# Second layer of a two-layer decoder: merged outputs kept in the query tiles, five rotating homes for cache keys and values, merges spread over the decode batches, residual split tile by tile

## What is computed

```python
def combine_groups(outs, lses):
    wts = jax.nn.softmax(jnp.stack(lses, axis=0), axis=0)
    return jnp.einsum('gnts,gntsd->ntsd', wts.astype(outs[0].dtype), jnp.stack(outs, axis=0))
```

## Time and profile before

| | |
|---|---|
| median of 3 runs | 2571.18 us (2569.72 to 2571.59) |
| the profiled execution | 2568.12 us |
| its span, first to last instruction | 2566.3 us |
| busy: PE, PEld, DVE, ACT, POOL | 2458.2, 2369.6, 1005.3, 657.2, 366.7 us |
| mean granted TensorE clock | 0.988 of full |
| DMA | 186.7 MB, mean 73 GB/s |
| stretch from the first sample score to oB | 1561.88 to 1702.56 us |

### The profile page before, as it was taken

One profiled execution on the slowest core, in us unless ns is written; L12 is line 12 of the kernel. 1 busy time (PEld: TensorE's weight loads), 2 busy tenths in 40 slices (PEclk: granted clock), 3 DMA queues, 4 the chain that ended last, 5 costly groups with the idle time before them and its releaser, 6 DMA issues. The chain is left out here.

```text
span 2566.3 us, 41256 instructions
## 1 busy us (share of the span) xinstructions
PE 2458.2 (96%) x16803; PEld 2369.6 (92%) x16803; DVE 1005.3 (39%) x1911; ACT 657.2 (26%) x1247; POOL 366.7 (14%) x242
## 2 busy tenths in 40 slices
PE   8999899999999999999999997689999999999997
PEld 8887799999999999999999775479999999999997
DVE  6566536322332232236212485436322322323235
ACT  4345324211110111123100493124211111111123
POOL 4333101101100101101111202201101100100100
PEclk9999999999999999999999999899999999999999
DMA  4011214113111313111211233523113111311312
GB/s 173 21 52 36 69 50 141 43 37 120 41 39 56 101 34 121 42 36 49 91 66 35 99 106 102 188 93 115 49 36 107 53 35 47 114 32 54 111 34 85
DMA packets 64943, 186.72 MB, mean 73 GB/s; under 512 B 11288, under 2 KB 17816, under 8 KB 64056
## 3 DMA queue, kind: packets, MB, share of 16 engines
q1 hardware_dynamic: 63928, 180.46, 21.7%
q0 software_dynamic: 912, 4.85, 0.5%
HBM read 175.85 MB, written 44.70 MB: 86 GB/s over the span
## 5 line engine op out<-in xcount | busy, mean ns | idle before, releaser
L969 DVE TENSOR_TENSOR WL<-RAW,WH 128x1024 fp32r<-128x1024 f32 (+3 forms) x196 | 216.4, 1105 | 1147.7 <-ACT WH L632 1147.1
L1508 PE MATMUL PS<-XH,WH 128*128 128x384 f32 x2832 | 621.0, 329 | 5.5 <-DVE XL L996 3.2
L1508 PE MATMUL PS<-XH,WL 128*128 128x384 f32 (+1 forms) x2736 | 603.5, 328 | 0.0
L1508 PE MATMUL PS<-XL,WH 128*128 128x384 f32 x2640 | 581.7, 328 | 0.0
L1508 PEld LDWEIGHTS PS<-XH,WH 128*128 128x128 f32 x2832 | 484.0, 188 | 7.3 <-issue 4.3
L632 ACT CAST WH<-RAW 128x1024 fp32r<-128x1024 f32 (+3 forms) x196 | 184.8, 944 | 1164.0 <-PE PS L1508 1149.1
L1508 PEld LDWEIGHTS PS<-XH,WL 128*128 128x128 f32 x2736 | 467.6, 188 | 0.0
L496 POOL TENSOR_TENSOR RAW<-RAW,GAIN 128x1024 f32<-128x1024 f32 x112 | 225.9, 2019 | 1663.7 <-DMA RAW<-in_w_gu 1418.7
L1508 PEld LDWEIGHTS PS<-XL,WH 128*128 128x128 f32 x2640 | 450.7, 188 | 0.0
L1508 PE MATMUL PS<-HL,WH 128*128 128x384 f32 (+1 forms) x1041 | 228.6, 327 | 0.0
L1508 PE MATMUL PS<-HH,WL 128*128 128x384 f32 (+1 forms) x1041 | 228.5, 327 | 0.0
(11 more groups left out here) (222 smaller groups left out, 2355.5 us busy)
## 6 DMA issues: line engine op xcount, KB each, us to landing
RAW<-in_w_gu SPq DMA_DIRECT2D x88, 512.0 KB, 3.5
out_bkS<-in_bk_in SPq DMA_DIRECT2D x8, 2032.0 KB
out_bvS<-in_bv_in SPq DMA_DIRECT2D x8, 2032.0 KB
RAW<-in_w_dn SPq DMA_DIRECT2D x32, 384.0 KB, 3.0
KC<-in_bk_in SPq DMA_DIRECT2D x8, 1536.0 KB, 10.9
VC<-in_bv_in SPq DMA_DIRECT2D x8, 1536.0 KB, 7.6
RAW<-in_w_dn SPq DMA_DIRECT2D x32, 320.0 KB, 2.9
XT<-in_xT SPq DMA_DIRECT2D x16, 544.0 KB, 4.8
```

Source lines behind the costliest of these rows:

```text
L969: nc.vector.tensor_tensor(lo[:, j, 0:nk * P], RAW[:, j, 0:nk * P], hi[:, j, 0:nk * P].bitcast(F32), ALU.subtract).then_inc(S["wl"], 1)
L1508: ins = mm(PS[:, 3 * j + c, 0:width], w[:, j, k * P:(k + 1) * P], x(k, a, width), start=(k == 0 and n == 0), stop=(k == nk - 1 and n == 2))
```

## The change

- The twelve tiles of QB grow from 1024 to 1088 columns; QNB goes, and the sample queries stand in the last 64 columns of their query tile. QBR is the same memory as fp32r. The key area moves up by 3072 bytes.
- The merged outputs are no longer written to XH. For a head pair p the tiles of groups 1 and 2 take the high and the low part once their products have been added (`outputs(QBR, 1)` and `outputs(QBR, 2)`); the sample outputs go to their last 64 columns. oB reads them there (`part(1)`, `part(2)`).
- KC and VC of all batches rotate through five homes outside the query tiles: KC0, VC0, KC1, VC1, ... take home 0, 1, 2, 3, 4, 0, ... Loads from the sixth on wait for the scores or values of the batch that used the home (`sb_pv` b-2 for keys, `sb_s` b-1 for values). VC0 and KC1 are asked for when the values of call C2 are done, VC1 and KC2 when the prompt's attention is done.
- The order by hand becomes one loop over the 8 batches on each engine. Batch b carries merge unit (b // 2, b % 2), the two rows of groups 0 and 1 before its values and the third behind them. `merge_hi` and `merge_lo` take a whole head pair (1024 columns) every second batch, the last pair after the loop.
- The TSN copies go; the mask is read from TSW at a constant offset.
- oB's slabs make XH and XL tile by tile (`split=True`); `after_o` isn't called for it, `release` isn't either, and both next slabs are prefetched.
- DVE waits for its own copy of VNB before it goes on to the queries.

```diff
@@ tiles
-        QB = at("QB", [P, 12 * SEQ], R)
-        KB = at("KB", [P, 4 * SEQ], R + 49152)
-        QNB = at("QNB", [P, 12, NEW], R + 65536)
+        QB = at("QB", [P, 12 * TOK], R)
+        QBR = at("QBR", [P, 12 * TOK], R, F32R)
+        KB = at("KB", [P, 4 * SEQ], R + 52224)
...
-        TSN = at("TSN", [P, NG, NEW], R + 79872)
-
-        KC = [at("KC0", [P, 4, KEPT], R + 49152), at("KC1", [P, 4, KEPT], o_wh + 4096), at("KC2", [P, 4, KEPT], R + 12288)]
-        VC = [at("VC0", [P, 6, 512], o_xl), at("VC1", [P, 6, 512], R), at("VC2", [P, 6, 512], R + 24576)]
+
+        HOMES = (R + 52224, o_xh + 16384, o_xl, o_wh + 4096, o_xh)
+        KC = [at(f"KC{b}", [P, 4, KEPT], HOMES[2 * b % 5]) for b in range(NEWB)]
+        VC = [at(f"VC{b}", [P, 6, 512], HOMES[(2 * b + 1) % 5]) for b in range(NEWB)]
...
+        def outputs(x, part):
+
+            return x[:].rearrange("p (a g n) -> p a g n", a=4, g=NG)[:, :, part]
@@ SP
+            def cache_in(n):
+
+                x, src = (KC, keys_of) if n % 2 == 0 else (VC, values_of)
+                sp.dma_start(x[n // 2][:], src(n // 2)).then_inc(S[f"home{n % 5}"], 16)
...
             sp.wait_ge(S["score"], C2)
-            values_in(0)
+            sp.wait_ge(S["pv"], C2)
+            cache_in(1)
+            cache_in(2)
             sp.wait_ge(S["ttr"], 64)
             sp.dma_start(TSB[:], t["tabSB"]).then_inc(S["tsb"], 16)
...
             sp.wait_ge(S["tr"], 2 * C3)
             sp.wait_ge(S["pv"], C3)
-            keys_in(1)
-            sp.wait_ge(S["sb_s"], 1)
-            keys_in(3)
-            sp.wait_ge(S["sb_pv"], 1)
-            values_in(3)
-            sp.wait_ge(S["c_lo"], 2)
-            values_in(1)
-            sp.wait_ge(S["c_lo"], 4)
-            keys_in(2)
-            sp.wait_ge(S["c_lo"], 6)
-            values_in(2)
-            for b in range(4, NEWB):
-                sp.wait_ge(S["sb_s"], b - 2)
-                keys_in(b)
-                sp.wait_ge(S["sb_pv"], b - 2)
-                values_in(b)
+            cache_in(3)
+            cache_in(4)
+            for n in range(5, 2 * NEWB):
+                b = n // 2
+                if n % 2 == 0:
+                    sp.wait_ge(S["sb_pv"], b - 2)
+                else:
+                    sp.wait_ge(S["sb_s"], b - 1)
+                cache_in(n)
             slabs("oB", t["w_oB"])
@@ POOL
+            for b in range(NEWB):
+                if b + 2 < NEWB:
+                    sample(b + 2)
+                pool.wait_ge(S["sb_stage"], 2 * min(b + 3, NEWB))
+                add(b // 2, b % 2)
+                pool.wait_ge(S["c_add"], 2 * b + 2)
@@ ACT
+            for b in range(NEWB):
                 if b + 1 < NEWB:
                     sample(b + 1)
-                if b + 1 == NEWB:
-                    act.wait_ge(S["sb_s"], NEWB)
+                sample_keys(b)
+                sample_norm(b)
+                if b and b % 2 == 0:
+                    merge_hi(b // 2 - 1)
+                sample_out(b)
+                if b == NEWB - 2:
+                    act.wait_ge(S["sb_pv"], NEWB - 1)
                     act.wait_ge(S["rows_out"], 80)
                     start("oB")
-                sample_keys(b)
-                sample_norm(b)
-                sample_out(b)
-            t_phase("oB", evac_sq(3, "oB"))
-            after_o(3, "oB")
+            merge_hi(3)
+            t_phase("oB", evac_sq(3, "oB", split=True))
@@ DVE
+            for b in range(NEWB):
                 if b + 1 < NEWB:
                     sample(b + 1)
-                if b + 1 == NEWB:
+                else:
                     start("oB")
+                    merge_product(b // 2, b % 2, 0)
+                    merge_product(b // 2, b % 2, 1)
+                sample_keys(b)
                 sums(b)
-                sample_keys(b)
+                for g in range(NG):
+                    if b + 1 < NEWB or g == 2:
+                        merge_product(b // 2, b % 2, g)
                 sample_out(b)
+                if b and b % 2 == 0:
+                    merge_lo(b // 2 - 1)
+            merge_lo(3)
             dve.wait_ge(S["rows_out"], 80)
-            t_phase("oB", evac_res(3, late=True), peel=True)
-            after_o(3, "oB")
+            t_phase("oB", evac_res(3, split=True), peel=True)
+            add_squares(3, KT - 1, 1)
+            low(3, KT - 1)
@@ PE
+            for b in range(NEWB):
+                p, h = b // 2, b % 2
                 if b + 1 < NEWB:
                     sample_scores(b + 1)
-                sample_turn(b)
+                    sample_turn(b)
+                    merge_row(p, h, 0)
+                    merge_row(p, h, 1)
+                else:
+                    merge_row(p, h, 0)
+                    merge_row(p, h, 1)
+                    sample_turn(b)
                 sample_values(b)
+                merge_row(p, h, 2)
                 sample_out(b)
-            pe.wait_ge(S["c_lo"], 8)
+            pe.wait_ge(S["c_lo"], 4)
             pe.wait_ge(S["sb_ol"], 16)
-            t_phase("oB", tiles(XH), tiles(XH, 4), None, release=True)
+            part = lambda z: lambda k, a, n: QBR[:, (NG * k + z) * TOK + a:(NG * k + z) * TOK + a + n]
+            t_phase("oB", part(1), part(2), None)
```

More of the change, by code:

```diff
@@ L640, in pair @@
                             split_hi(name, 2 * i + j + 2, j)
-                        elif prefetch and PLAN.next(name) and not (j and name in ("oA", "oB")):
+                        elif prefetch and PLAN.next(name) and not (j and name == "oA"):
                             split_hi(PLAN.next(name), j, j)
@@ L1340, in coefficients, with merge_product, merge_lo @@
                 ins.then_inc(S["coef"], 1)
-            def merge_products(p, h):
-                for g in range(NG):
-                    n = 3 * (2 * p + h) + g
-                    dve.wait_ge(S["c_t"], n + 1)
-                    x = natural(g, p, h)
-                    nc.vector.tensor_tensor(x, x, as_tokens(PS[:, 2 * (n % 2), :], g), ALU.mult).then_inc(S["c_mul"], 1)
-            def merge_lo(p, h):
-                n = 2 * p + h
-                dve.wait_ge(S["c_hi"], n + 1)
-                at, to = q_at(0, p) * SEQ + 512 * h, p * TOK + 512 * h
-                nc.vector.tensor_tensor(XH[:, 4 * TOK + to:4 * TOK + to + 512], QB[:, at:at + 512],
-                                        XH[:, to:to + 512].bitcast(F32), ALU.subtract).then_inc(S["c_lo"], 1)
+            def merge_product(p, h, g):
+                n = 3 * (2 * p + h) + g
+                dve.wait_ge(S["c_t"], n + 1)
+                x = natural(g, p, h)
+                nc.vector.tensor_tensor(x, x, as_tokens(PS[:, 2 * (n % 2), :], g), ALU.mult).then_inc(S["c_mul"], 1)
+            def merge_lo(p):
+                dve.wait_ge(S["c_hi"], p + 1)
+                nc.vector.tensor_tensor(outputs(QBR, 2)[:, p, 0:SEQ], outputs(QB, 0)[:, p, 0:SEQ],
+                                        outputs(QBR, 1)[:, p, 0:SEQ].bitcast(F32), ALU.subtract).then_inc(S["c_lo"], 1)
             dve.wait_ge(S["tsb"], 32)
@@ L1873, in sample_scores, with merge_row @@
                 ins.then_inc(S["sb_s"], 1)
-            def merge_rows(p, h):
+            def merge_row(p, h, g):
                 pe.wait_ge(S["coef"], 1)
-                for g in range(NG):
-                    n = 3 * (2 * p + h) + g
-                    if n >= 2:
-                        pe.wait_ge(S["c_mul"], n - 1)
-                    for x in range(4):
-                        for kk in range(2):
-                            c = CW[:, g, 4 * h + x, 2 * p + kk:2 * p + kk + 1].to_broadcast([P, HD])
-                            ins = mm(PS[64 * kk:64 * kk + 64, 2 * (n % 2), x * P:(x + 1) * P], c, IDN[:], start=True, stop=True)
-                    ins.then_inc(S["c_t"], 1)
+                n = 3 * (2 * p + h) + g
+                if n >= 2:
+                    pe.wait_ge(S["c_mul"], n - 1)
+                for x in range(4):
+                    for kk in range(2):
+                        c = CW[:, g, 4 * h + x, 2 * p + kk:2 * p + kk + 1].to_broadcast([P, HD])
+                        ins = mm(PS[64 * kk:64 * kk + 64, 2 * (n % 2), x * P:(x + 1) * P], c, IDN[:], start=True, stop=True)
+                ins.then_inc(S["c_t"], 1)
             def sample_turn(b):
```

143 lines of the change are left out of this document (21 added, 122 removed).

## The result

The kernel after takes 2527.41 us (median of 4 runs, 2525.73 to 2531.24) beside 2571.39 for the kernel before (4 runs, 2569.72 to 2572.30): ratio 0.983, 95% interval 0.9817 to 0.9842. The prediction was 2527.7 us. The profiled execution is one of 2526.71 us, with a span of 2524.9 and a mean clock of 0.994 (before 2568.12, 2566.3 and 0.988).

What follows compares the result with a forecast made beforehand. PE is busy 96% of the span, so only its waits before oB and behind it can give time. Terms: -40.1 + 0.6 - 4.0 = -43.5 from 2568.12, so 2524.6, median 2527.7 us; range 2521 to 2541.

Steps and rivals of the forecast that it cites:

- What bounds the stage: First sample score to oB: loads and products make PE wait; afterwards PE's own work fills each step, 10.9 us.
- The two delays of 1.25 us: Steps of batches 2 and 4: `merge_lo`, behind a POOL addition, delays the next minima; 2.5 us in all.
- Step 7: Last batch: two rows 1.98, turn to values 4.06, values 1.87, third row 0.99; 8.9 us.
- 6, where the next step asks for no minima: Batch 6: `merge_lo` there was to delay nothing, as no minima follow; 0 us.
- Step 0: First batch, from scores(0) at 1561.88 to the next step's start at 1580.0, with 0.5 us for the clock.
- End chain: Behind the last third row, PE waits for product, addition, `merge_hi`, `merge_lo` and hops before oB; 5.7 us.
- The ramp: Start of oB: after 5 us idle it may run longer at the lower clock; +0.6 us, bounds 0 and 4.
- The seam: oB's end to gu10's first slab: with the residual split tile by tile nothing is lost; -4.0 us, bounds -4 and 0.
- no idle time behind XL: gu10's first slab: a sign of being right, PE not waiting there for XL tiles.
- load took the place of the merge wait: Rival, scores 3 to 7: keys land late, steps of 16.6 or 13.3 us, time 2556 or 2540; chance 0.08.
- The chain: Rival, steps: hops between rows and products and POOL overlaps cost +7, 2535; no own chance, counted in the forecast's range.
- the lower clock: Rival, whole stage: PE at 1.2 GHz, 2597 us, chance 0.04; for two or three steps 2538 to 2548, chance 0.06.

Runs made afterwards that it cites:

- the old seam: Kernel after with the end of oB as before (no tile-by-tile split, `after_o` and `release` back, second slab not prefetched): 2529.81 us, ratio 0.9836.
- second set of runs: Kernel after, unchanged, five runs on one chip beside the version with all repairs: 2530.18 us, ratio 0.9840.

## Why the prediction was right, point by point

**What bounds the stage.** Right. Before, the loads waited for merges and the merges for products; with both waits gone PE's own work is the step (busy 10.64 of 10.82 us; 10.9 predicted). That the keys have 12.2 us from request to use and that this is enough was right; shifted by one step it is not, as the late requests show. One sign was set wrong: PE was to be busy above 90% of the stage, and nearly the 96.5 us of before. It was busy 85.63 us, 86%. The prediction's own waits come to about 12 of 100.6 us, so 90% did not fit its sum, and the 96.5 held the slow clock.

**The two delays of 1.25 us.** Right in place and cause, and 1.03 in size: the addition had begun 0.26 us before `merge_lo`, so less than its whole length was left, and `merge_lo` is 1.15 us longer and not 1.31. By the Trainium skill (SBUF — State Buffer, Who interferes with whom) a VectorE instruction with two SBUF inputs and a reading GpSimd instruction exclude each other for a whole instruction, and the one issued first goes first. The trace agrees, on both sides: 1.22 to 2.37 for the difference that comes second, 1.53 to 2.31 for the addition that comes second. The 2 x 1.1 us that the prediction worked out by that rule came nearer than the 2 x 1.25 that it summed. The products, of which one input comes from PSUM, are not touched: with the merges bunched one takes 0.69 us, the shortest seen, in the middle of an addition that takes its usual 1.52.

**Step 7, 8.9 us.** The step that failed: 9.96 to the end of the third row. "6, where the next step asks for no minima" was true and not the question. The next step asks for products and keys, and ahead of these stand in DVE's order a `merge_lo` of 2.35 and two weight splits of 1.28. I had costed ScalarE's `start("oB")` as hidden and had not followed DVE's, which is in the same place. From turn to values it took 4.99 us and not 4.06; the two rows took 2.14 and not 1.98. It is the stretched `merge_lo` that costs: with it moved and the splits left the wait is 0.75 us again, as in the kernel before. What failed is the nothing that the prediction put for `merge_lo` in step 6; the splits by themselves would have stayed hidden. The last out (0.33 us) runs inside the end chain.

**Step 0, 18.1 us.** 17.21. The 0.5 us for the clock was not needed in this execution, but other executions with the same code up to there have 12.2 to 12.3 in place of 11.57, with scores(1) at the lower clock: 17.8 to 18.0 in all. So the size of 18.1 fits those, and 0.9 too much here is partly the clock that did not fall.

**End chain, 5.7 us.** 5.43 from the end of the third row, 5.11 of it behind the last out, as its links were each about 0.1 shorter than their bounds.

**The ramp, +0.6 for oB after the idle time.** -0.36 here, and 49.2 to 50.05 us over the variants, against 49.63 before. Here oB's first six matmuls take 2.18 us and the later groups of six 1.16; the kernel before has such a slow stretch near oB's start too, behind an idle time of 1.09 us. Three profiles with 2.7 us of idle time before oB have 49.2 to 49.35, the ones with 5.11 have 49.27 to 50.04 (the kernel after itself 49.27 and 49.85). The ranges touch, so whether the longer idle time costs anything these profiles leave open; none of them goes beyond the 50.2 predicted.

**The seam, -4.0.** -2.28, and the sign "no idle time behind XL" was not met (1.44 us); the mechanism is right (with the old seam 2.8 us come back), the term was taken at its bound. The sum of DVE's work per slab (4.9 us) left room, but it was a mean: at the end two of DVE's instructions with two SBUF inputs fall on POOL's scalings of gu10's slabs (2.56 us for 1.21, 2.98 for 1.28), and the weight split stands ahead of the last residual. The prediction counted 6.5 us for tile 7's chain from oB's end; from 1713.06 to the end of XL, 1725.09, it took 12.0.

**The rivals.** No load took the place of the merge wait: the landing is 7.9 us at the median, and the late requests show what the case would have looked like. The chain (a microsecond more a step) didn't come either. Nor did the lower clock, in this kernel (1.00 in the steps 0 to 7; it falls only in the idle time before oB). In the three variants in which PE waits more inside the steps (merges bunched, keys late, no merge) it did, with scores at 1.93 us, the lower level of 1.2 GHz, and their stages came out 7.5, 5.2 and 1.6 us above what I had expected from the waits. The rule on transposes that the prediction took from the Trainium skill (TensorE: Matmul & The Clock Gate, Part 4: PE-mode transpose) would have favoured the lower clock. The page says it of the transpose mode, and the turns here are plain matmuls; a step with 3.3 us of them in 10.8 ran at 1.00, so for these the trace does not bear it out.

**The sum.** -43.5 against -41.4 between the profiles and -43.98 between the medians. That the predicted median, 2527.7 us, lies 0.3 from the measured one is luck. In the profiled execution the misses cancel only in part: 1.0 too much in the stage and 0.9 in oB, against 1.7 too little in the slab and 2.3 of scatter ahead of the stage, 2.1 too little in the sum. The remaining 2.1 are made good because the median stands only 0.7 above the profiled execution, where the prediction had added 3.1. The second set of runs has 2530.18.

## What to carry to other kernels

When buffers are freed by a side task, look where they lie before making the task faster: with the homes out of its way, and scores(1) ahead of the first rows, half of the gain was there, and spreading the task so that PE always has its own work ahead of a wait gave the other half, in part through the clock. For every instruction that an engine does late in a step, list what stands behind it on its own queue, not only the link that you have in mind. And before a VectorE operation with two SBUF inputs is put in place, see what GpSimd does at that time: the same instruction costs 1.2 or 2.4 us.

## What the runs showed of the hardware that I had not expected

- A wait costs more than its length. Late key loads gave 5.4 to 6.1 us of idle time a step. The first step with such a wait at its end took 16.26 us, its 10.9 and the wait; the four behind it, which begin with the scores after a wait, took 18.2 to 19.6, where 10.82 plus the idle time is 16.2 to 16.9. Those scores took up to 4.6 us in place of 2.41.
- The clock of identical code differs between executions (1.00 against 0.97 over 1400 to 1500 us). Across eleven profiles of the kernel after and its variants (scores(0) from 1562.3 to 1567.0 us), with one code up to that point, the start of the stage moves by 4.7 us. Changes of 1 to 3 us were to be seen in the intervals of the trace and not in the medians.
- The exclusion works in the direction of who began first. `merge_lo` 0.26 us behind an addition took 2.37 us, and PE waited for what stood behind it; 0.30 us ahead of one it took 1.23, and the addition 2.31, for which nothing waited.
